# One round order for another in the prompt attention: turns, weights and scores on TensorE, splits before the maximum on VectorE

## The reference, cut to what matters

```
s   = q . kc * scale            # 16 compressed blocks; softmax over the valid ones; o_cmp = p @ vc
s2  = q . k_selected * scale    # top 16 blocks of 64; here all 16 blocks exist, so all keys up to the query
p2  = softmax(s2);  o_slc = p2 @ v_selected
s3  = q . k_window * scale      # the last 512 keys
p3  = softmax(s3);  o_win = p3 @ v_window
o_att = gate0 * o_cmp + gate1 * o_slc + gate2 * o_win
```

## Time and profile before

| | us |
|---|---|
| median of 2 runs | 2829.82 (2828.55 to 2831.1) |
| profiled execution, its own time | 2830.15 |
| its span | 2828.5 |
| TensorE busy | 2554.1 (90%) |
| VectorE busy | 975.9 |
| ScalarE busy | 662.5 |
| GpSimd busy | 1194.0 |

### The profile page before, as it was taken

The page is one execution under the profiler, slowest core; times in us unless marked ns, Lnnn a source line. Parts: engine busy times, 40 slices in busy tenths (PEclk is TensorE's granted clock), DMA queues, the critical chain, the costliest instruction groups (busy, mean ns, idle before and its releaser), DMA issues.

```text
span 2828.5 us, 50789 instructions
## 1 busy us (share of the span) xinstructions
PE 2554.1 (90%) x20106; PEld 1741.1 (62%) x20106; DVE 975.9 (35%) x1440; ACT 662.5 (23%) x1438; POOL 1194.0 (42%) x885
## 2 busy tenths in 40 slices
PE   7999999999969898866675999999969999999997
PEld 3666666666649854554443666666636666666665
DVE  2322222311085433866532442222172223232104
ACT  3311111101052243755430011111251111111002
POOL 2378787834333330100022884444334434443431
PEclk9999999999989955999997999999989999999998
DMA  6133333321102431000033332211101111121111
GB/s 233 38 97 95 97 95 98 100 62 41 50 8 54 146 99 36 2 1 1 1 97 100 104 101 57 55 45 56 46 15 54 51 52 52 45 60 52 51 31 60
DMA packets 298368, 179.52 MB, mean 63 GB/s; under 512 B 8847, under 2 KB 288773, under 8 KB 298176
## 3 DMA queue, kind: packets, MB, share of 16 engines
q1 hardware_dynamic: 282780, 156.15, 18.9%
q0 software_dynamic: 3840, 11.54, 1.4%
q10 hardware_dynamic: 11620, 10.04, 1.1%
HBM read 170.81 MB, written 11.10 MB: 64 GB/s over the span
## 4 chain that ended last, share of the span: by engine, by line
PE 74%; issue 13%; DVE 6%; ACT 3%; POOL 2%; DMA 1%; SPq 0%; POOLq 0%; ACTq 0%; DVEq 0%
PE banks L224 23%; PE banks L225 23%; PE banks L226 22%; PE banks L1481 2%; ACT pair L521 1%; DVE rs L577 1%; PE banks L320 1%; ACT ahi L524 1%; PE banks L2217 1%; DVE y L594 1%; POOL orow L1865 1%; POOL opart L1862 1%; DVE pair L617 0%; PE banks L461 0%; DVE alo L607 0%
## 5 line engine op out<-in xcount | busy, mean ns | idle before, releaser
L224 PE MATMUL banks<-ahi,whi 128*128 128x344 f16 x2784 | 865.9, 311 | 26.9 <-ACT sg L876 14.4
L225 PE MATMUL banks<-alo,whi 128*128 128x344 f16 x2784 | 865.8, 311 | 0.0
L226 PE MATMUL banks<-ahi,wlo 128*128 128x344 f16 x2784 | 865.7, 311 | 0.0
L215 POOL TENSOR_SCALAR stage<-stage 128x1024 f32<-128x1024 f32 (+1 forms) x248 | 273.6, 1103 | 975.3 <-PE banks L226 907.0
L220 POOL TENSOR_TENSOR wlo<-stage,whi 128x1024 f16<-128x1024 f32 (+1 forms) x248 | 545.8, 2201 | 20.6
L224 PEld LDWEIGHTS banks<-ahi,whi 128*128 128x128 f16 x2784 | 273.8, 98 | 165.2 <-issue 16.2
L226 PEld LDWEIGHTS banks<-ahi,wlo 128*128 128x128 f16 x2784 | 273.9, 98 | 136.5
L225 PEld LDWEIGHTS banks<-alo,whi 128*128 128x128 f16 x2784 | 273.9, 98 | 133.4 <-issue 0.4
L224 PE MATMUL banks<-hhi,whi 128*128 128x344 f16 x1056 | 326.3, 309 | 3.2 <-DVE hlo L937 3.2
L225 PE MATMUL banks<-hlo,whi 128*128 128x344 f16 x1056 | 326.3, 309 | 0.0
L226 PE MATMUL banks<-hhi,wlo 128*128 128x344 f16 x1056 | 326.3, 309 | 0.0
(11 more groups left out here) (320 smaller groups left out, 3765.8 us busy)
## 6 DMA issues: line engine op xcount, KB each, us to landing
stage<-in_w_ffn_gu_dram SPq DMA_DIRECT2D x88, 512.0 KB, 3.9
stage<-in_w_ada_dram SPq DMA_DIRECT2D x56, 512.0 KB, 3.8
stage<-in_w_ffn_down_dram SPq DMA_DIRECT2D x32, 704.0 KB, 4.7
stage<-in_w_in_dram SPq DMA_DIRECT2D x38, 512.0 KB, 3.8
first<-in_w_ada_dram SPq DMA_DIRECT2D x4, 2048.0 KB, 12.8
xrow<-in_x_prompt_dram ACTq DMA_DIRECT2D x8, 512.0 KB, 7.1
stage<-in_phi_w_dram SPq DMA_DIRECT2D x8, 512.0 KB, 3.8
ring<-in_state_win_kv_dram SPq DMA_DIRECT2D x16, 256.0 KB, 3.3
```

The costliest lines, as they stand in the source:

```text
L215: pool.tensor_scalar(st, st, WS, 1.0, ALU.mult, ALU.mult).then_inc(slab_scaled, 1)
L224: pe.matmul(out, w_hi, a_hi, start=start, stop=False)
L225: pe.matmul(out, w_hi, a_lo, start=False, stop=False)
L226: return pe.matmul(out, w_lo, a_hi, start=False, stop=stop)
```

## The change

It writes the round in another order, and moves the compressed units. On TensorE the turn of u - 2 and the product of u - 4 now stand ahead of the scores of u; on VectorE the split of u - 3 stands ahead of the maximum of u; on ScalarE the exponent is that of u - 1. A compressed unit is turned, split and multiplied one round later than before, behind the scores, and its shares two rounds after its scores. RL, the delay of a tile's last transposes, is 5 instead of 4. The wait of the maximum for an earlier exponent now names that of unit u - 4, whose place in `stat` it takes.

```diff
-                    if u >= 4:
-                        dve.wait_ge(S("p_exp"), at("p_exp") - 2)
+                    if u - 4 in prob_ready and units[u - 4][0] != "cmp":
+                        dve.wait_ge(S("p_exp"), prob_ready[u - 4][1])
...
-        RL = 4
+        RL = 5
         for u in range(U + PL + RL + 2):
-            def unit(back):
-                return u - back if 0 <= u - back < U else None
+            def unit(back, compressed):
+
+                v = u - back
+                return v if 0 <= v < U and (units[v][0] == "cmp") == compressed else None
...
-            if unit(0) is not None:
-                score_unit(u)
-            if unit(TL) is not None:
-                turn(u - TL)
-            if unit(PL) is not None:
-                weighted(u - PL)
+            if unit(TL, False) is not None:
+                turn(u - TL)
+            if unit(PL, False) is not None:
+                weighted(u - PL)
+            if u < U:
+                score_unit(u)
+            if unit(TL + 1, True) is not None:
+                turn(u - TL - 1)
+            if unit(PL + 1, True) is not None:
+                weighted(u - PL - 1)
             if row_end(PL + RL) is not None:
                 rows_turn(row_end(PL + RL))
-            if unit(PL + 1) is not None and units[u - PL - 1][0] == "win" and units[u - PL - 1][2] % 2 == 1:
-                pair_shares(u - PL - 1)
-            if unit(0) is not None:
-                greatest(u)
-            if unit(EV) is not None:
+
+            if unit(EV, False) is not None:
                 turned_hi(u - EV)
...
+            v = unit(PL + 1, False)
+            if v is not None and units[v][0] == "win" and units[v][2] % 2 == 1:
+                pair_shares(v)
+            if unit(EV, False) is not None:
                 turned_lo(u - EV)
+            if u < U:
+                greatest(u)
+            if 1 <= u <= U:
+                exponent(u - 1)
+            if unit(2, True) is not None:
+                compressed_shares(u - 2)
```

More of the change, by code:

```diff
@@ L1903, in _ @@
                                   oahi[:, :, t * P:(t + 1) * P], ALU.subtract).then_inc(S("t_lo"), 1)
-        RL = 4
+        RL = 5
         for u in range(U + PL + RL + 2):
-            def unit(back):
-                return u - back if 0 <= u - back < U else None
+            def unit(back, compressed):
+                v = u - back
+                return v if 0 <= v < U and (units[v][0] == "cmp") == compressed else None
             def row_end(back):
-                v = unit(back)
+                v = unit(back, False)
@@ L1921, in mixer @@
+            if unit(PL + 1, True) is not None:
+                weighted(u - PL - 1)
             if row_end(PL + RL) is not None:
                 rows_turn(row_end(PL + RL))
-            if unit(PL + 1) is not None and units[u - PL - 1][0] == "win" and units[u - PL - 1][2] % 2 == 1:
-                pair_shares(u - PL - 1)
-            if unit(0) is not None:
-                greatest(u)
-            if unit(EV) is not None:
+            if unit(EV, False) is not None:
                 turned_hi(u - EV)
-            if unit(PL + 1) is not None and units[u - PL - 1][0] == "cmp":
-                compressed_row(units[u - PL - 1][1])
+            if unit(EV + 1, True) is not None:
+                turned_hi(u - EV - 1)
@@ L1931, in mixer @@
+            if unit(PL + 2, True) is not None:
+                compressed_row(units[u - PL - 2][1])
             if row_end(PL + RL + 1) is not None:
                 rows_hi(row_end(PL + RL + 1))
[L1933 to L1937, removed]
-                turned_lo(u - EV)
+            v = unit(PL + 1, False)
+            if v is not None and units[v][0] == "win" and units[v][2] % 2 == 1:
+                pair_shares(v)
```

## The result

The changed kernel takes **3082.08 us** (median of two runs, 3080.36 to 3083.8) against 2829.82: a ratio of **1.0891**, with a 95% interval of 1.0865 to 1.0918. That is 252 us more, where I had forecast 15 more. The profiled execution took 3083.8 us, its span is 3082.1 us, and the mean granted clock of TensorE over the span fell from 0.945 to 0.883.

A forecast was written before the change was run, and what follows sets the result against it. VectorE was taken to bound tile 3, and a loop of waits tiles 4 to 7. The terms 11.8 + 11.9 - 2.4 - 3 - 2.8 = +15.5 on 2829.8 gave 2845 us, range of 8 in 10 2825 to 2866.

The forecast's parts named there:

- The steady round of tiles 4 to 7: 0: Plain rounds of tiles 4 to 7: the loop stays 2.90 us and exponents come in time, so no change.
- The step on the tiles with one bank a unit: Tiles 0 to 3: turn and product now stand before the next scores, +11.9 us, of which 3.7 in tile 3.
- The clock, left out of the sum: TensorE's granted clock in the attention: kept for the range only, from 6 us gained to 22 us lost.
- The last rival: Slower by over 2%: gaps bring half speed in all 64 rounds of tiles 4 to 7, +88 us, chance 0.03.
- the other terms: All terms of the sum besides the steady round's 0: 11.8 + 11.9 - 2.4 - 3 - 2.8 us.
- VectorE's 2.4: Tiles 0 to 3: part of a compressed unit's nine small VectorE operations now falls into waits, -2.4 us.
- 11.8: Tiles 4 to 7: a pair's shares now stand ahead of the split that the ring waits for, 16 x 0.74 us.
- the two credits: Tiles 4 to 7: -3 us at the change of tile and -2.8 us at the end, where one round falls away.
- The split really is free of the maximum: Rival: rounds of tiles 4 to 7 lose the maximum from their loop, 47 to 60 us, 2770 to 2783, chance 0.04.
- Nothing changes: Rival: shares slip into gaps and the change of tile gives back more, 2822 to 2834 us, chance 0.16.
- the clock costs some: Rival: longer gaps lower the clock, 10 to 22 us on top of 2845, 2856 to 2868, chance 0.14.

The follow-up runs named there:

- own-maximum kernel: The changed kernel with each exponent waiting for its own unit's maximum instead of the newest one: 2851.72 us, ratio 1.0074.
- The experiment with early shares: The changed kernel with each exponent waiting for its own maximum, and a pair's shares one round earlier, between split and maximum on VectorE: 2830.18 us.
- The experiment with the split first: The kernel before with one edit, on VectorE the split of u - 3 ahead of the maximum of u: 2863.87 us, ratio 1.0121.
- the fill: The changed kernel with five extra 512-column matmuls, output thrown away, ahead of the turn's wait for the exponent: 3008.39 us, ratio 1.0631.

## Why the prediction was wrong

**The failed step** is in "The steady round of tiles 4 to 7: 0", and in its words: "What is new is that the turn of u - 2 must find its exponent ready after one unit's scores and not two. An exponent starts 0.71 after its maximum ... so it is in time." I took the 0.71 of the earlier trace rows as a property of the exponent. It was a property of the place where its wait was written. The printed orders of both kernels name the semaphore that an instruction waits for, not the value, and I went by the names. The diff showed `exponent(u - 1)` behind `greatest(u)`, and the function's one line with `at("s_max")` was in the code all the time. What the runs showed in its place: the exponent is late for its turn nearly everywhere, 104 waits of TensorE, 1.92 us in the round shown; the steady round is 4.98 and not 2.90, and tiles 4 to 7 take 155.8 us more, where this term said 0. That step alone is most of the 252 us. With the wait mended it holds: 2.95 a round and exponents in time, in the own-maximum kernel.

**The step on the tiles with one bank a unit** has the same fault: its chain of 3.02 for two units begins with the maximum to the exponent, 0.71. With the newest maximum a single unit takes 3.15, and tile 3 went from 27.1 to 61.2. With the own maximum it takes 30.60, where I had said 30.

**The clock, left out of the sum.** The last rival had the mechanism (a gap at every round, gaps of about 2 us), and gave it a chance of 0.03 and a price of 88 us. The gaps came, from a wait that I had not seen, and the clock fell with them. At least 74 of the 252 us are its work. What I had not seen is that ring and clock feed each other: a longer ring makes the gap, with the gaps TensorE's granted clock fell to 0.62, and that makes TensorE's links of the ring longer. In tiles 4 to 7 the same instructions keep TensorE busy 238.41 us here and 155.31 in the own-maximum kernel. My reading that before the change only waits near 2.75 were followed by a low clock was not right either. In that trace one wait of 2.88 (to 1320.07) left it at 1.00 in the 3 us that followed, and from 1388 to 1394 it stood at 0.50 around a wait of 1.96 (to 1391.21): the length of a single wait does not decide it.

**What held, once the wait is mended.** The sum of the other terms was +15.5, and the own-maximum kernel is 21 us over the kernel before. By windows, against the earlier trace rows: tiles 0 to 2 +8.7 where the terms say 8.2, less a share of VectorE's 2.4; tile 3 +3.5 for 3.7; tiles 4 to 7 +11.2 for 11.8 - 3 - 2.8 = 6. The experiment with early shares tells which term of tiles 4 to 7 was off. With the shares out of the way these tiles are 6.1 us shorter than before, and the two credits together said 5.8. The shares' place, with the clock that goes with it, is worth 17.3 there and not 11.8. The delay itself is as I had it, 1.49 - 0.74 = 0.75 for each of 16 pairs in the timeline, 12 us. The other 5 went with a granted clock of 0.93 with the shares late and 0.97 with them early; that the clock is their cause is likely and not shown. In tiles 0 to 3 VectorE's credit of 2.4 did not come: with early shares they still take 4.4 more than before. All this rests on one profiled execution of each kernel, so single microseconds in it say little.

**The rivals.** "The split really is free of the maximum", 2770 to 2783, was argued away with the words that in a queue's cycle neither thing is first. That argument is right for the changed kernel, whose scores stand between the turns as before. It says nothing about what the maximum's departure is worth, and here 47 to 60 us was a fair size: where it does leave the loop, the runs are 61 and 59 us shorter, all of it in tiles 4 to 7. But the prediction knew of one ring only. The experiment with the split first found a second, through ScalarE, with rounds of 3.07 in tile 4 and 2.62 in tile 3, and 2863.87 in all. "Nothing changes" did not decide anything; "the clock costs some" may be the 5 us in the own-maximum kernel. The case with the largest price was in none of the rivals: that an exponent could wait for a maximum that it doesn't need.

**What stays open.** How the 230 us divide between ring and clock beyond the 74 that the fill gave back; the filled kernel still pays for its own fill. What each credit of tiles 4 to 7 was by itself. And what the late exponent with its own maximum is worth without the split first.

## What to carry to other kernels

When a call is moved in code whose waits are read off a running count, its wait moves too: write down, for each moved instruction, the value that it waits for and which unit's signal that is, before and after, and let each unit keep its own number. Then draw every ring across the engines' queues, not only the one through the bound engine, and add up the links of each; an order pays only once all rings longer than the target are open, so that an edit which loses alone (the split first, 33 us here) can be half of one that wins 59. Look at stages apart: this edit lost 41 us in tiles 0 to 3 and gained 7 in tiles 4 to 7. If a ring is left with gaps on TensorE in every round, price the clock with it, since a low clock lengthens TensorE's links of that ring.

## What the runs showed of the hardware

Waits of 1.7 to 1.9 us in every round of 3 to 5 us went with a mean granted clock of 0.62 over 573 us. Waits of 1.1 us in rounds of 2.9 us, with one of 1.85 at each pair's shares, left it at 0.93 over tiles 4 to 7. Between them lies the kernel with the split first, with 0.80 in tile 3, whose rounds are 2.62. I had not expected so much to hang on the difference. The window of the round shown of the changed kernel, and of the one before it, has both levels in it (1.2 GHz in the first):

```profile
1376.30:1381.30 5.00, 3.51 (x25) 2.29 (x25) 1.20 (x4) 1.54 (x4) 0.00 (x0) 0.50 0.02 3
1381.30:1386.28 4.98, 2.52 (x26) 1.63 (x26) 1.71 (x4) 1.54 (x4) 0.00 (x0) 0.84 0.00 0
```

Nearly the same work of TensorE, 25 and 26 matmuls, takes 3.51 us in the one and 2.52 in the other. Nor had I expected that matmuls whose result is thrown away would be worth having: five of them a unit took 74 us, 2.4%, off the changed kernel, though TensorE's queue is the one in the ring. Closing the gap is worth far more: mending the wait gave 230.
